# A decoder trunk on one core: A's queries and keys projected straight into features on partitions, and ScalarE scaling the probabilities of B, C and A

## The reference

```
u = RMSNorm(h); proj = u @ w_in                      # 4008 columns, split over four branches
A: q = rmsnorm(c_q) @ w_uq -> 4 heads x (64 + 32)    # c_q 192 wide, last 32 rotated
   kv = rmsnorm(c_kv) @ w_ukv -> 4 heads x (64 + 64) # c_kv 128 wide
   k_rope: 32 rotated columns, shared by the heads; softmax((qk) / sqrt(96)) @ v, causal
B: dilated attention, 4 heads, three patterns merged, position bias
C: an indexer of 8 heads picks 128 keys for each query; 4 heads attend over them, position bias
D: differential attention, 4 heads of two maps, p0 - lambda * p1, then a norm
y = concat(A, B, C, D, each * silu(gate)) @ w_out; h = h + RMSNorm(y)
```

## Time and profile before

| | us |
|---|---|
| runs | 775.15, 771.83, 767.22 |
| median | 771.83 |
| the profiled execution | 768.9 |
| its span | 767.0 |
| mean granted TensorE clock | 0.954 |

### The profile page before, as it was taken

How to read it: one execution, slowest core, us unless ns; L and a number is a source line. 1 busy time by engine, 2 the same in 40 slices (tenths; PEclk the granted TensorE clock), 3 DMA queues, 4 the chain that set the end, 5 groups by cost and what they waited for, 6 DMA issues and landing times. The chain is left out here.

```text
span 767.0 us, 10353 instructions
## 1 busy us (share of the span) xinstructions
PE 690.5 (90%) x3836; PEld 553.9 (72%) x3836; DVE 450.4 (59%) x1067; ACT 328.7 (43%) x750; POOL 218.4 (28%) x91
## 2 busy tenths in 40 slices
PE   3996999998989899889998999999898989988996
PEld 2885877787776674448997887788787767444896
DVE  4211597987688645561182158888978864556214
ACT  4422534654223445571434345456432344457221
POOL 1332241424035430200335342324323543020020
PEclk9998999997899976999999999999999997699999
DMA  8457963423122110202353487542322221020112
GB/s 259 123 188 233 258 185 111 124 76 106 55 69 69 69 56 1 109 1 80 96 157 111 129 254 228 157 138 69 98 70 68 70 70 56 0 108 3 43 42 110
DMA packets 66753, 81.47 MB, mean 106 GB/s; under 512 B 10720, under 2 KB 52320, under 8 KB 66703
## 3 DMA queue, kind: packets, MB, share of 16 engines
q1 hardware_dynamic: 66703, 80.81, 34.2%
HBM read 70.28 MB, written 13.93 MB: 110 GB/s over the span
## 5 line engine op out<-in xcount | busy, mean ns | idle before, releaser
L694 POOL TENSOR_TENSOR w_low<-w_raw,w_high 128x2048 fp32r<-128x2048 f32 (+2 forms) x39 | 175.8, 4507 | 435.3 <-ACT w_high L733 435.3
L1215 PE MATMUL bank<-uT,w_high 128*128 128x512 f32 x400 | 161.2, 403 | 0.0
L1217 PE MATMUL bank<-uT,w_low 128*128 128x512 f32 x400 | 159.2, 398 | 0.0
L1216 PE MATMUL bank<-uT,w_high 128*128 128x512 f32 x400 | 159.1, 398 | 0.0
L837 ACT ACTIVATE probs<-probs,negmax 128x128 f32<-128x128 f32 (+3 forms) x160 | 89.1, 560 | 99.6 <-DVE negmax L1070 99.0
L1215 PEld LDWEIGHTS bank<-uT,w_high 128*128 128x128 f32 x400 | 76.2, 190 | 18.7 <-issue 1.9
L1217 PEld LDWEIGHTS bank<-uT,w_low 128*128 128x128 f32 x400 | 76.2, 190 | 18.0
L1216 PEld LDWEIGHTS bank<-uT,w_high 128*128 128x128 f32 x400 | 76.3, 191 | 16.5
L733 ACT ACTIVATE w_high<-w_raw 128x2048 fp32r<-128x2048 f32 (+2 forms) x40 | 74.7, 1868 | 29.8 <-DMA w_raw<-in_w_out 23.7
L1215 PE MATMUL bank<-w_high,mix 128*128 128x256 f32 x256 | 72.4, 283 | 1.0 <-DVE mix L1155 1.0
L1216 PE MATMUL bank<-w_low,mix 128*128 128x256 f32 x256 | 71.6, 280 | 0.0
(11 more groups left out here) (145 smaller groups left out, 1119.0 us busy)
## 6 DMA issues: line engine op xcount, KB each, us to landing
w_raw<-in_w_in SPq DMA_DIRECT2D x28, 1024.0 KB, 5.4
w_raw<-in_w_out SPq DMA_DIRECT2D x8, 1024.0 KB, 4.9
parts_dram<-staging SPq DMA_DIRECT2D x12, 512.0 KB, 5.9
strips<-strips_dram SPq DMA_DIRECT2D x24, 256.0 KB, 4.6
dqk<-parts_dram SPq DMA_DIRECT2D x24, 256.0 KB, 4.3
hX<-in_x SPq DMA_DIRECT2D x8, 512.0 KB, 5.8
strips_dram<-table_dram SPq DMA_DIRECT2D x1, 3328.0 KB
qidx<-parts_dram SPq DMA_DIRECT2D x12, 256.0 KB, 4.2
```

The source lines that it names most:

```text
L694: nc.gpsimd.tensor_tensor(w_low[:, s, :, 0:w], w_raw[:, s, :, 0:w], w_high[:, s, :, 0:w].bitcast(F32), ALU.subtract).then_inc(w_low_done, 1)
L1215: nc.tensor.matmul(out_ap, lh, rh, start=start, stop=False)
L1216: nc.tensor.matmul(out_ap, lh, rl, start=False, stop=False)
L1217: return nc.tensor.matmul(out_ap, ll, rh, start=False, stop=stop)
```

## The change

Two parts, in one diff.

1. For the jobs of B, C and A the step `norm` on VectorE keeps only the reciprocal; ScalarE waits for it and scales the four row blocks in place by copies with a per-partition scale. TensorE's turns wait for ScalarE (`probs_scaled`) instead; D is as before (`maps_joined`).
2. A's `aup` and `aturn` steps are replaced. `aq` h: a head's queries, 128 features on partitions by 512 tokens (64 plain, 32 rotary, and the same 32 with halves swapped), two products; ScalarE copies the 64 plain rows and VectorE multiplies the other 64 by a table of cosines and sines. The product over 128 rows of query and key then adds the two halves of the rotation. The token's root isn't multiplied into the queries: VectorE's shift of A's scores has it as its factor (`negroot`). `aroot`: the key latent's roots, spread over all partitions by four products with the identity, are multiplied into `latkv` on VectorE. `ak`: keys of two heads in one product, two ScalarE copies; `av`: values of two token blocks, one ScalarE copy. The rotary key is rotated on GpSimd at norm 8 with rows that SyncE loads, and SyncE stores it into both places of every head at norm 9. The transpose of it in `aup_head` goes, and the weights of A are loaded in eight transfers instead of three.

```diff
-             10: [("aup", 0), ("aup", 1), ("aturn", 0)],
-             11: [("aup", 2), ("aturn", 1), ("aup", 3), ("aturn", 2), ("aturn", 3)]}
+             10: [("aq", 0), ("aq", 1), ("aroot",), ("aq", 2)],
+             11: [("aq", 3), ("ak", 0), ("ak", 1), ("av", 0), ("av", 1)]}
...
                 if step == ("norm", 3):
-                    sp.dma_start(wuq[:, 0, :], mla_w_uq[l, 0:P, :]).then_inc(a_loaded, 16)
-                    sp.dma_start(wuq[0:QL - P, 1, :], mla_w_uq[l, P:QL, :]).then_inc(a_loaded, 16)
-                    sp.dma_start(wukv[:], mla_w_ukv[l]).then_inc(a_loaded, 16)
+                    half = A_ROPE // 2
+                    for c, (first, n) in enumerate(((0, P), (P, QL - P))):
+                        cols = mla_w_uq[l, first:first + n, :].rearrange("p (h d) -> p h d", h=HEADS)
+                        sp.dma_start(wuq[0:n, c, :, 0:A_QK], cols).then_inc(a_loaded, 16)
+                        sp.dma_start(wuq[0:n, c, :, A_QK:A_QK + half], cols[:, :, A_QK - half:A_QK]
+                                     ).then_inc(a_loaded, 16)
+                        sp.dma_start(wuq[0:n, c, :, A_QK + half:P], cols[:, :, HD:HD + half]).then_inc(a_loaded, 16)
+                    kv = mla_w_ukv[l].rearrange("p (h t d) -> p t h d", h=HEADS, t=2)
+                    for t in range(2):
+                        sp.dma_start(wukv[:, t, :].rearrange("p (h d) -> p h d", h=HEADS), kv[:, t]
+                                     ).then_inc(a_loaded, 16)
+                    sp.wait_ge(scores_ready, l * NS + NS_IDX)
+                    sp.dma_start(trig[HD:P, :], rope).then_inc(trig_loaded, 16)
+                if step == ("norm", 8):
+                    sp.wait_ge(bias_ready, (l + 1) * HEADS)
+                    wait_unit_emptied(sp, l * NU + UNIT_AT[("unit", "cq", 1)])
+                    sp.dma_start(trig2[HD:A_QK, :], rope[A_ROPE:2 * A_ROPE, :]).then_inc(krx_loaded, 16)
+                    sp.dma_start(krx[HD:HD + 16, :], latq[HD + 16:A_QK, 1, :]).then_inc(krx_loaded, 16)
+                    sp.dma_start(krx[HD + 16:A_QK, :], latq[HD:HD + 16, 1, :]).then_inc(krx_loaded, 16)
+                if step == ("norm", 9):
+                    sp.wait_ge(kr_ready, l + 1)
+                    sp.wait_ge(scores_ready, l * NS + NS_IDX + S_AT[8])
+                    for first in (HD, A_QK):
+                        sp.dma_start(aqk[first:first + A_ROPE, 1, :, :],
+                                     latq[HD:A_QK, 1, :].unsqueeze(1).to_broadcast([A_ROPE, HEADS, SEQ])
+                                     ).then_inc(krope_loaded, 16)
...
@@ GpSimd @@
+                if step == ("norm", 8):
+                    pool.wait_ge(trig_loaded, 16 * (l + 1))
+                    pool.wait_ge(krx_loaded, 48 * (l + 1))
+                    pool.wait_ge(w_low_done, lows[0])
+                    pool.wait_ge(roots_ready, ROOT_AT[l, ("dsquares", 1)] + 1)
+                    pool.wait_ge(bias_ready, (l + 1) * HEADS)
+                    raw, turn = latq[HD:A_QK, 1, :], krx[HD:A_QK, :]
+                    nc.gpsimd.tensor_tensor(raw, raw, trig[HD:A_QK, :], ALU.mult).then_inc(kr_step, 1)
+                    pool.wait_ge(kr_step, 2 * l + 1)
+                    nc.gpsimd.tensor_tensor(turn, turn, trig2[HD:A_QK, :], ALU.mult).then_inc(kr_step, 1)
+                    pool.wait_ge(kr_step, 2 * (l + 1))
+                    nc.gpsimd.tensor_tensor(raw, raw, turn, ALU.add).then_inc(kr_ready, 1)
+                    pool.wait_ge(kr_ready, l + 1)
...
@@ ScalarE @@
+                if kind == "norm" and MAPS[step[1]] == 1:
+                    j = step[1]
+                    buf = probs[probs_buffers(j)[0]]
+                    act.wait_ge(inv_ready, scaled(l, j))
+                    for q in range(NB):
+                        pr = buf[:, POFF[q]:POFF[q] + WID[q]]
+                        ins = nc.scalar.activation(pr, pr, ACT.Copy, scale=inv[:, j % 4, 0, q:q + 1])
+                    ins.then_inc(probs_scaled, 1)
...
+                if kind == "aq":
+                    n = l * NU + UNIT_AT[step]
+                    act.wait_ge(unit_ready, n + 1)
+                    nc.scalar.activation(aqk[0:HD, 0, step[1], :], bank[0:HD, unit_bank(n), :], ACT.Copy
+                                         ).then_inc(high_written, 1)
+                if kind == "ak":
+                    n = l * NU + UNIT_AT[step]
+                    act.wait_ge(unit_ready, n + 1)
+                    for half in range(2):
+                        ins = nc.scalar.activation(aqk[0:HD, 1, 2 * step[1] + half, :],
+                                                   bank[HD * half:HD * (half + 1), unit_bank(n), :], ACT.Copy)
+                    ins.then_inc(emptied_by["act"], 1)
+                if kind == "av":
...
+                    nc.scalar.activation(values[0][:, 2 * i:2 * i + 2, :].rearrange("p t c -> p (t c)"),
+                                         bank[:, unit_bank(n), :], ACT.Copy).then_inc(emptied_by["act"], 1)
...
@@ VectorE @@
+                    ins.then_inc(maps_joined, 1)
                 else:
-                    after(nc.vector.reciprocal(inv[:, i, 0], sums[:, i, 0]))
-                    for q in range(NB):
-                        sl = slice(POFF[q], POFF[q] + WID[q])
-                        ins = nc.vector.tensor_scalar(probs[bufs[0]][:, sl], probs[bufs[0]][:, sl],
-                                                      inv[:, i, 0, q:q + 1], None, ALU.mult)
-                ins.then_inc(probs_ready, 1)
+                    nc.vector.reciprocal(inv[:, i, 0], sums[:, i, 0]).then_inc(inv_ready, 1)
...
+                        scale = negroot[:, q:q + 1] if br == "A" else -1.0
...
+                if kind == "aroot":
...
+                    nc.vector.tensor_tensor(latkv[:], latkv[:], bank[:, unit_bank(n), :], ALU.mult
+                                            ).then_inc(emptied_by["dve"], 1)
+                if kind == "aq":
...
+                    dve.wait_ge(high_written, highs(n))
+                    nc.vector.tensor_tensor(aqk[HD:P, 0, step[1], :], bank[HD:P, unit_bank(n), :], trig[HD:P, :],
+                                            ALU.mult).then_inc(emptied_by["dve"], 1)
...
@@ TensorE @@
+                if kind == "aq":
+                    h = step[1]
+                    pe.wait_ge(a_folded, l + 1)
+                    b = work_bank(l * NU + UNIT_AT[step])
+                    nc.tensor.matmul(b, wuq[:, 0, h, :], latq[:, 0, :], start=True, stop=False)
+                    nc.tensor.matmul(b, wuq[0:QL - P, 1, h, :], latq[0:QL - P, 1, :], start=False, stop=True
+                                     ).then_inc(unit_ready, 1)
+                if kind == "aroot":
...
+                    for tb in range(NB):
+                        ins = nc.tensor.matmul(b[:, tb * P:(tb + 1) * P],
+                                               roots[:, r, NB + tb:NB + tb + 1].to_broadcast([P, P]), ident[:],
+                                               start=True, stop=True)
+                    ins.then_inc(unit_ready, 1)
+                if kind == "ak":
+                    wait_unit_emptied(pe, l * NU + UNIT_AT[("aroot",)])
+                    b = work_bank(l * NU + UNIT_AT[step])
+                    nc.tensor.matmul(b, wukv[:, 0, step[1] * P:(step[1] + 1) * P], latkv[:], start=True, stop=True
+                                     ).then_inc(unit_ready, 1)
+                if kind == "av":
+                    b = work_bank(l * NU + UNIT_AT[step])
+                    for half in range(2):
+                        tb = 2 * step[1] + half
+                        ins = nc.tensor.matmul(b[:, half * 256:(half + 1) * 256], latkv[:, tb * P:(tb + 1) * P],
+                                               wukv[:, 1, :], start=True, stop=True)
+                    ins.then_inc(unit_ready, 1)
```

More of the change, by code:

```diff
@@ L241, in units_of @@
         return ["dve"]
-    if k == "aup_head":
-        return ["dve", "dve"]
-    if k == "aup":
-        return ["dve", "act"]
-    if k == "aturn":
-        return ["act", "act"]
+    if k in ("aup_head", "aq", "aroot"):
+        return ["dve"]
+    if k in ("ak", "av"):
+        return ["act"]
     return []
@@ L338, in convert_steps @@
         for s in STEPS[freed + 1:]:
-            cost += {"unit": 1 if s[0] == "unit" and GROUPS[GI[s[1]]][2] else 2, "aup": 1, "pv": 1}.get(s[0], 0)
+            cost += {"unit": 1 if s[0] == "unit" and GROUPS[GI[s[1]]][2] else 2, "aq": 1, "ak": 1, "pv": 1}.get(s[0], 0)
             if cost >= CONVERT_AFTER.get(g, 4):
@@ L391, in trunk @@
         room("wukv", 2 * KB)
-        room("wuq", 3 * KB)
-        room("small", 4 * KB)
+        room("wuq", 4 * KB)
+        room("small", 3 * KB)
         w_raw = at("w_raw", "raw", [P, SLOTS, KC, GW], F32)
@@ L1056, in _ @@
                     br, h = JOBS[j]
+                    if br == "A" and h == 0:
+                        dve.wait_ge(negroot_ready, l + 1)
                     if br != "A":
@@ L1069, in _ @@
```

(7 more changed lines are left out.)

140 lines of the change are left out of this document (41 added, 99 removed).

## The result

The changed kernel takes 793.88 us (median of 4 runs, 789.28 to 797.98) beside 772.50 us for the kernel before on the same chip (4 runs). The ratio is 1.0284, with a 95% interval of 1.0201 to 1.0367: slower. All ratios here are taken over executions within 1.5% of the fastest of the same kernel, while the medians are over all of them, so the two can differ, most where many were slower (five of ten in the kernel before with 128 rows, three of six in the last kernel). The profiled execution took 795.84 us, with a span of 794.1 us and a mean granted clock of 0.924; before it was 0.954.

A forecast was written before the change was run, and what follows sets the result against it. TensorE bounds the kernel, by its work, its granted clock and its stalls. Stalls and work summed to +3.85 us a layer, with the clock +8.25, twice +16.5, giving 785.4 and a named 787 us; range 766 to 802.

The forecast's parts named there:

- The copies: Four ScalarE scaling copies per job: estimated at 1.9 us, bounds 1.3 and 2.4.
- bv 2, pv 4, job 7, pv 5: TensorE waits per layer: bv 2 grows to 4.9 us, pv 4 to 3.6, job 7's 2.80 goes, pv 5 late by 0.75.
- pv 6: Stall of 1.54 us at 305.28: +2.1 us a layer, from norm 10's copies and the emptying of query 2.
- A's jobs: ScalarE's queue, norms 11 to 15: copies fill its idle hole and set the pace, together +3.8 us a layer.
- Stalls in A's turns, ak 1: Stalls of 0.78 and 1.20 us go (-2.0 a layer); ak 1 waits for query 3's bank (+0.5).
- The key rows: A's rotary key rows via GpSimd and SyncE: there at 285, before A's scores after 319.26, so cost 0.
- The clock: Half clock after new stalls at bv 2 and pv 4, less job 7's, plus A's stretch: +4.4 us a layer, bounds -7 and +11.
- A's stretch: Half-clock stretch beginning in aup_head, 16.90 us from 282.90: lasts 3.4 us longer, costing +1.7 us a layer.
- The 6.8 us behind job 7's stall: Half clock from 264 to 273: goes in two cases of three, worth -2.3 us a layer.
- rival 3: Clock worse: half until pv 6 in both layers, third drop at pv 6 or among A's jobs; 803 us, chance 0.10.
- Rival 1: Clock stays as it is, only stalls and work change: 779.5 us, chance 0.20.
- Rival 2: Not slower: long query products bring the clock back soon, new stalls go unpunished; 764.7 us, chance 0.20.

The follow-up runs named there:

- the kernel before with 128 rows: The kernel before, second product of each query pair run over 128 rows instead of 64, added rows holding zeros: 766.87 us, ratio 0.9823.
- the last kernel: A's projection, job 7 alone scaled on ScalarE, 128-row query pairs, turned blocks and bv 0's and bv 1's values copied ahead of exponentials: 739.94 us, ratio 0.9617.
- Part 2 alone: The changed kernel with all scaling back on VectorE, so only A's new projection differs from the kernel before: 766.37 us, ratio 0.9879.
- the late copies: The changed kernel with ScalarE's scaling copies of jobs 5, 6 and 10 moved further down its queue: 772.80 us, ratio 1.0033.
- job 7 alone on ScalarE: A's projection as changed, only job 7 scaled on ScalarE, the rest on VectorE: 760.40 us, ratio 0.9845; with 128-row query products 750.21 us, 0.9767.

## Why the prediction was right, and where its sizes were off

The sign and the likeliest case held: 793.9 us lies in the forecast's own range of 779 to 796, at its upper end, 7 us over the 787 named. The mechanism was right in the main, and some of the agreement is luck. Term by term:

- **The copies.** Estimated at 1.9 us for four, between 1.3 and 2.4; measured 1.90, the row at 224.28.
- **bv 2, pv 4, job 7, pv 5.** Forecast 4.9, 3.6, none and 0.75; measured 4.80, 3.52, none and 0.71. That the copies slip in ahead of the very instruction that TensorE waits for is shown by the kernel in which they were moved: 3.00 and 1.71 again.
- **pv 6.** Forecast +2.1 to 3.64; measured 4.51. The step named the emptying of query 2 by both engines but gave it almost nothing (2.1 in all, of which 1.9 for the copies). Part 2 alone shows what it costs: 2.71 us without one copy, 1.17 more than before, by the rows at 302.00 to 303.69.
- **A's jobs.** Forecast +3.8 in ScalarE's queue. Of TensorE's stalls of 0.6 us and more from 320 to 360 the sum is 6.5 us (1.72, 1.27, 1.52, 1.32, 0.65) against 3.4 before (0.62, 0.78, 1.95): +3.1. The pace, read between the third exponentials of jobs 14 and 15, was to go from 6.2 to 6.9 us; they stand at 342.41 and 349.74 now, 7.3 apart, with 3.4 us of half clock in between.
- **Stalls in A's turns, ak 1.** -2.0 and +0.5: gone, and 0.45.
- **The key rows**, costed at 0 with 285 us as their time: GpSimd's last product of them ended at 281.2, and nothing waits. At 1.28 us each the products are as estimated (1.3).
- **The weights' fold**, not in the sum at all: 1.33 us in the second layer (the row at 669.02), and 1.72 in the first layer of part 2 alone. This wait was not seen. The fold of `wukv` stands behind a 2.51 us product of VectorE at 665.26, and the first query product waits for it though it reads only `wuq`.

Together the idle terms gave 1.9 + 1.9 - 2.05 + 2.1 + 3.8 - 2.0 + 0.5 = 6.15 a layer, 12.3 us in all; measured 12.2. That the sum fits so well is luck: two misses of opposite sign, pv 6 (+0.9) and A's jobs (-0.7), nearly cancel, and the fold was left out.

**The clock** is the term that was mis-sized. Busy time was to change by 2 x (4.4 - 2.3) = +4.2 us and changed by +14.9. Half clock behind bv 2 and pv 4 came as said, 6.8 us each in the first layer; in the second only 3.4 each, though the stalls are the same. A's stretch was to be 3.4 us longer, and so it is, 20.5 instead of 17.1 in both layers. The 6.8 us behind job 7's stall went in both layers, as said for two cases of three. These named places sum to 13.6 us more at half, where the forecast had counted about 25. Missing from the sum are the drops of 3.4 to 6.8 us behind pv 6 and among A's jobs, five in the two layers and 20.5 us together; the third drop of rival 3, which had a chance of 0.10, stood for them. A further 13.7 us at half stand from 563.9 on, behind the counterpart of the stall at 182.30 in the second layer. The kernel before has that stall in both layers and the half clock behind it only in the first; in others of these kernels it stands in both, with the change and without, so it is not put down to the change. So the forecast's clock term failed in both directions: too much for the places it named, nothing for the drops behind pv 6 and among A's jobs; and up to 7 us of the measured difference, half of those 13.7, are a stretch that other kernels show without the change.

**The rivals.** Rival 1, the clock untouched, is out: the clock is 0.50 behind both long stalls, and feeding TensorE ahead of the waits brought it back. Rival 2 said that long query products bring the clock back soon. They didn't in the changed kernel, with 64 rows in every other one; with 128 rows they did, and that kernel's 777.9 us is near rival 1's time. The forecast had named a right cause for the length of A's stretch, the alternation of 128 and 64 rows, and sized what the change adds to it rightly; it didn't see that the kernel before pays for the same thing. Four pairs of kernels that differ in the rows (and, in all but the kernel before, in a wait for the rotary key that ends early) show the cost, by the ratios: 1.4% in the changed kernel, 1.2% with the late copies, 0.8% with job 7 alone on ScalarE and 1.8% in the kernel before, 6 to 14 us. In the third pair the intervals overlap.

The Trainium skill (TensorE: Matmul & The Clock Gate, What's actually happening) says that activity releases the throttle. The timeline of the changed kernel has 8 us of query products one on the other, from 289.96 on, at 0.50 throughout. The page's sentence doesn't say why there, where with 128 rows, and once with 64, the clock came back within them. Why the added rows bring the clock back no run here shows; that the kernel is faster with them, four pairs show. Zeros in the added rows of both operands weren't tried: the first 32 of one always held the rotary key.

## What to carry to other kernels

Before work is moved to a less busy engine, look at what stands behind it in that engine's queue: here 1.90 us of copies cost 1.8 us of TensorE at each of two places, plus the clock, while moving a quarter of the copies a few instructions back gave nine tenths of it back. Compare with the right kernel too: beside the projection alone even the well-placed copies cost about 1%. Move an operation where its old engine is held up (1.9 instead of 7.16 us at job 7), not for the average. And where TensorE stays at half clock through a run of products that use a part of the rows, try filling the weights' other rows with zeros: a product takes no longer for it, and the clock may come back.

## What was not expected of the hardware

A run of products with 64-row contractions in it can stay at half clock though TensorE had no gap (20.50 us busy of 20.50 in the first layer); with the rows filled up, 20.5 us at 0.50 became 6.8 and 10.2. Giving TensorE 20 products more didn't make a kernel slower but, it seems, 7 to 8 us faster, 786.1 against 793.9. A stall of 3.00 us at bv 2 costs no clock in the profile of the kernel before, and 3.4 us at half in that of the late copies; 4.80 us at the same place cost 6.8 us at half in one layer and 3.4 in the other. Executions of one kernel differ by the drops that they catch: the fastest kernel ranges from 728.7 us, with a clock of 0.983, to 745.1.
